# Two chained transformer blocks on one core: woven matmuls ahead of a pair's row products from row 290 on, another order of work before the first expert gather, a third norm buffer, and tables loaded early

## The reference

```python
def first_block(x, c, ctx, ...):               # x: 512 x 1024
    sh1, sc1, gt1, sh2, sc2, gt2 = ada_mod(c, ada_w, ada_b)
    ...
    o = jnp.concatenate([o_gdn, o_rwkv], axis=-1) @ w_out
    x = x + gt1 * o[:, n_ctx:]
    x = x + gt2 * peer_ffn(modulate(rms_norm(x, norm2_g), sh2, sc2), ...)
    return rms_norm(x, final_norm_g)

def peer_ffn(h, w_query, sub_keys, down, up):
    q = (h @ w_query).reshape(B, T, 8, 2, 128)          # 16 queries a token
    s = jnp.einsum('bthpd,hpkd->bthpk', q, sub_keys)    # 128 scores each
    s_top, i_top = lax.top_k(s, 16)
    ...                                                 # best 16 of 16 x 16 sums, 8 heads
    gate = jax.nn.softmax(best_s, axis=-1)              # 128 experts a token
    act = gelu(einsum('td,ted->te', h_blk, down[i_blk]))
    return einsum('te,ted->td', act * g_blk, up[i_blk]) # a block of 128 tokens
```

## Time and profile before

| | us |
|---|---|
| median of 3 runs | 3761.59 (3760.1 to 3765.12) |
| the profiled execution, its own time | 3768.46 |
| its span, first to last instruction | 3766.4 |
| PE busy | 3306.8 (88%) |
| DVE busy | 2408.0 (64%) |
| ACT busy | 1114.4 (30%) |
| POOL busy | 1014.9 (27%) |

### The profile page before, as it was taken

How to read it: one execution, slowest core, us unless ns; L and a number is a source line. 1 busy time by engine, 2 the same in 40 slices (tenths; PEclk the granted TensorE clock), 3 DMA queues, 4 the chain that set the end, 5 groups by cost and what they waited for, 6 DMA issues and landing times.

```text
span 3766.4 us, 59546 instructions
## 1 busy us (share of the span) xinstructions
PE 3306.8 (88%) x24177; PEld 1947.6 (52%) x24177; DVE 2408.0 (64%) x4781; ACT 1114.4 (30%) x2905; POOL 1014.9 (27%) x1021
## 2 busy tenths in 40 slices
PE   7998899899998876666567999999999998999998
PEld 4556666788876332222122333333368854468853
DVE  3865635687756766588777787764444147457765
ACT  2442212444422332333334344332222023410000
POOL 1024410345420333333342233323200000034432
PEclk8999999999999999777788999999999999999999
DMA  4147630000024999999999999989834421012233
GB/s 184 45 184 264 226 113 23 2 11 3 3 86 145 383 414 417 415 405 415 403 414 373 357 389 375 375 344 388 333 108 145 132 74 43 1 68 90 90 123 145
DMA packets 146412, 800.88 MB, mean 213 GB/s; under 512 B 13934, under 2 KB 33773, under 8 KB 62812
## 3 DMA queue, kind: packets, MB, share of 16 engines
q0 software_dynamic: 76048, 543.64, 36.1%
q1 hardware_dynamic: 68940, 251.34, 18.3%
q10 hardware_dynamic: 1152, 2.10, 0.1%
HBM read 794.92 MB, written 2.10 MB: 212 GB/s over the span
## 4 chain that ended last, share of the span: by engine, by line
PE 54%; DVE 13%; DMA 10%; ACT 4%; issue 2%; POOL 0%; DVEq 0%; POOLq 0%; ACTq 0%
PE bank L104 19%; PE bank L2721 8%; DMA row<-in_experts,idxs 7%; PE bank L3154 7%; PE bank L3170 4%; PE bank L4244 3%; DVE row L2914 3%; DMA wring<-in_experts,idxs 2%; PE bank L3946 2%; PE bank L2668 1%; PE bank L1108 1%; DVE wring L2914 1%; PE bank L1089 1%; PE bank L1880 1%; ACT cf L2811 1%
## 5 line engine op out<-in xcount | busy, mean ns | idle before, releaser
L2721 PE MATMUL bank<-row,dg 64*64 64x512 f32 x2920 | 431.8, 703 | 212.2 <-ACT dg L2817 211.8
L2914 DVE CUSTOM_DVE_ANT_0 row<-row,bank 128x1024 f32<-128x1024 f32 x365 | 445.6, 1221 | 192.4 <-DMA row<-in_experts,idxs 154.7
L2981 POOL DMA_INDIRECT row<-in_experts,idxs x365 | 362.3, 993 | 712.7 <-PE bank L2721 643.5
L2721 PEld LDWEIGHTS bank<-row,dg 64*64 64x64 f32 x2920 | 114.9, 148 | 470.6 <-issue 470.0
L3154 PE MATMUL bank<-s_hid,wring 128*128 128x512 f32 x704 | 327.3, 610 | 0.0
L104 PE MATMUL bank<-hT,wring 128*128 128x256 f32 (+1 forms) x864 | 286.6, 492 | 3.0 <-ACT sq L898 3.0
L2808 ACT ACTIVATE act<-dots 128x2 f32<-128x2 f32 x256 | 51.8, 203 | 710.6 <-DVE dots L2914 710.2
L2721 PE MATMUL bank<-wring,dg 64*64 64x512 f32 x1176 | 180.1, 708 | 91.0 <-ACT dg L2817 90.9
L2981 POOL DMA_INDIRECT wring<-in_experts,idxs x147 | 141.7, 964 | 368.7 <-PE bank L2721 264.3
L3154 PEld LDWEIGHTS bank<-s_hid,wring 128*128 128x128 f32 x704 | 129.0, 192 | 200.1 <-issue 199.3
L2914 DVE CUSTOM_DVE_ANT_0 wring<-wring,bank 128x1024 f32<-128x1024 f32 x147 | 179.5, 1221 | 81.0 <-DMA wring<-in_experts,idxs 67.5
(11 more groups left out here) (731 smaller groups left out, 6376.5 us busy)
## 6 DMA issues: line engine op xcount, KB each, us to landing
wring<-in_ffn_up SPq DMA_DIRECT2D x66, 1024.0 KB, 6.8
wring<-in_ada_w SPq DMA_DIRECT2D x64, 1024.0 KB, 6.6
wring<-in_ffn_down SPq DMA_DIRECT2D x32, 704.0 KB, 4.3
wring<-in_ffn_w_down SPq DMA_DIRECT2D x20, 1024.0 KB, 6.5
wring<-in_w_in SPq DMA_DIRECT2D x7, 2048.0 KB, 8.2
wring<-in_peer_w_query SPq DMA_DIRECT2D x8, 1024.0 KB, 25.6
wring<-in_attn_w_qkv SPq DMA_DIRECT2D x3, 2048.0 KB, 7.8
row<-in_experts,idxs POOLq DMA_INDIRECT x365, 9.9
```

Of the source, the lines that this page charges most:

```text
L2721: ins = pe.e.matmul(self.ks[t][64 * half:64 * half + 64, :], self.dg[u % 4][p, 0:64], row[p, 1024 + half * 512:1536 + half * 512], start=( ...
L2914: e.tensor_tensor_reduce(row, row, P.pairs[0], 1.0, 0.0, MUL, ADD, self.dots[:, g % 2, x:x + 1]).then_inc(*V.up("pg_dot", j))
L2981: e.indirect_dma_start(self.places[r], None, P.i["experts"], bass.IndirectOffsetOnAxis(ap=idu[:, b, j % 128:j % 128 + 1], axis=0)).then_in ...
```

## The change

It has three parts, which share no code.

**One: MixerOut.** PE turns only block 3 first, and does the w_out product of a block's half in two parts of 4 matmuls, the part of the first four input chunks (those of o_gdn) and that of the last four (out_pe's new argument `part`). Of block 2, half a column half stands ahead of the queries 0 to 7 (before: both halves), the rest behind them. DVE norms block 3 as before, then makes the first 8 choice steps, and only then adds block 2. Norms of the other blocks are split into `mean` and `normed`, and ACT's order goes with it. The query tiles get six places (an idle part of the constants, and y of the scan stage), so that all eight tiles are loaded without a place that waits for queries past the fourth tile.

**Two: Experts.pe.** For rows from 290 on, the woven work of a pair of rows stands ahead of the pair's row products; for rows before that, the steps of rest_pe of an even row move from behind the pair's products to ahead of them.

**Three: n10 and Qkv.** n10 has three buffers tmp (so that the third block needs none back), only two qkv units instead of four stand ahead of n10's turns, and the rest are followed by one turn each. The tables of the rotation and the gains have a place of their own and are loaded once the last block of the first stage is finished (pg_final 3), by POOL, which waited for the stage's begin before.

```diff
@@ MixerOut.dv
+        self.mean(dv, 3)
         self.normed(dv, 3)
         self.heads_dv(dv, 0)
+        choice, f = P.experts.choose(dv, 3, 0), self.first
+        for _ in range(8):
+            next(choice)
         self.added(dv, 2, 0)
+        next(choice)
         self.added(dv, 2, 1)
-        choice, f = P.experts.choose(dv, 3, 0), self.first
-        for _ in range(11):
+        for _ in range(2):
             next(choice)
         self.added(dv, 1, f)
...
+        self.mean(dv, 2)
         self.added(dv, 1, 1 - f)
         self.added(dv, 0, 1 - f)
-        for b in (2, 1, 0):
+        self.normed(dv, 2)
+        for b in (1, 0):
+            self.mean(dv, b)
+        for b in (1, 0):
             self.normed(dv, b)
@@ MixerOut.ac
         x.scores_ac(ac, 0, 7)
         x.rows_ac(ac, 0)
         x.weigh(ac, 3, 0)
+        self.squares(ac, 2)
+        self.root(ac, 2)
         for n in range(8, 16):
             x.query_ac(ac, 0, n)
             if n > 8:
                 x.scores_ac(ac, 0, n - 1)
+            if n == 8:
+                self.squares(ac, 1)
             if n == 9:
-                self.squares(ac, 1)
-            if n == 10:
                 self.squares(ac, 0)
-                self.root(ac, 2)
-            if n == 12:
                 self.root(ac, 1)
-            if n == 14:
                 self.root(ac, 0)
@@ MixerOut.out_pe
-    def out_pe(self, pe, ws, b, half):
+    def out_pe(self, pe, ws, b, half, part):
+
         P = self.P
         w, wb = ws[half]
-        k = P.bank(pe, "ro_o", half, b)
+        k = P.ps("ro_o", half, b) if part else P.bank(pe, "ro_o", half, b)
         pe.wait_ge(*P.at("wload", w))
-        pe.wait_ge(*P.at("free", "ro_T", b, 1))
...
+        pe.wait_ge(*P.at("free", "ro_T", b, part))
+        ins = mm(pe.e, k, [(self.oT[part][:, c, b * 128:(b + 1) * 128], wb[:, 4 * part + c, :]) for c in range(4)], start=(part == 0), stop=(part == 1))
+        if part:
+            ins.then_inc(*self.T.up("ro_o", half, b))
@@ Experts
-        self.wq = Tiles(P, "query_w", quarter[2:4] + [first[0], P.mem("wq", 2048)], 8)
+        self.wq = Tiles(P, "query_w", quarter[2:4] + [first[0], P.mem("wq", 2048), P.cst[:, P.idle:P.idle + 2048],
+                                                      P.rout.rs.y.rearrange("p b h i -> p (b h i)")], 8)
...
-        return 2 + n % 2 if n < 8 else n % 2
+        return (2, 3, 4, 2, 3, 4, 5, 2)[n] if n < 8 else n % 2
...
-        for n in range(16):
-            after = None if n < 2 or n in (8, 9) else n - 2
+        for n in (2, 0, 1, 3, 4, 5, 7, 6, 8, 9, 10, 11, 12, 13, 14, 15):
+            after = {3: 0, 4: 1, 5: 2, 7: 3}.get(n) if n < 10 else n - 2
...
-            if x % 2 == 0:
-                self.row_pe(pe, u)
-                self.row_pe(pe, u + 1)
             for _ in range(self.steps(u)):
                 next(rest, 0)
...
+            if u < self.BEHIND and x % 2 == 0:
+                self.row_pe(pe, u)
+                self.row_pe(pe, u + 1)
             P.around.pe(pe, u)
+            if u >= self.BEHIND and x % 2:
+                self.row_pe(pe, u - 1)
+                self.row_pe(pe, u)
+
+    BEHIND = 290
...
             elif r == 3:
-                po.wait_ge(*P.at("query_w_free", 6))
+                po.wait_ge(*P.at("query_w_free", 7))
@@ HiddenState, Tail.pe, Qkv
-        return self.tmps[n % 2], self.order[n - 2] if n >= 2 else None
+        return self.tmps[n % self.spare], self.order[n - self.spare] if n >= self.spare else None
...
-        P.cycle((1, 2, 3))
-        for u in range(1, P.qkv.ahead):
-            P.qkv.unit_pe(pe, u)
-        P.cycle((5, 6, 7, 4))
+        P.cycle((1,))
+        P.qkv.unit_pe(pe, 1)
+        P.cycle((5, 6, 7, 2, 3, 4))
         for b in (2, 3, 4):
             P.n10.turn_pe(pe, b)
...
-        super().po(po)
         i, e = self.P.i, po.e
+        po.wait_ge(*self.P.at("pg_final", 3))
...
-        for u in range(self.ahead, 14):
+        for u in range(2, 14):
             self.unit_pe(pe, u)
-            for _ in range(2 if u == self.ahead + 2 else 1):
-                self.turn(pe, turned)
-                turned += 1
-        for u in range(turned, 14):
+            self.turn(pe, u - 2)
+        for u in (12, 13):
             self.turn(pe, u)
```

More of the change, by code:

```diff
@@ L360, in plan @@
         self.top = hbase + 32960
-        self.n10 = HiddenState(self, 1, 0, "ffn0", "n10", "ffn0_down_x", 0, [5, 2, 3, 4])
+        self.n10 = HiddenState(self, 1, 0, "ffn0", "n10", "ffn0_down_x", 0, [5, 2, 3, 4], 3)
         self.top = low
@@ L2333, in added, with mean @@
         e.tensor_tensor(P.x[:, b, cs], P.x[:, b, cs], tp, ADD).then_inc(*V.up("x1", half, b))
+    def mean(self, dv, b):
+        st = self.st[:, 56 + 4 * b:60 + 4 * b]
+        dv.wait_ge(*self.P.at("pq_sq", b))
+        dv.e.tensor_scalar(st[:, 1:2], st[:, 0:1], 1.0 / D, 1e-6, MUL, ADD).then_inc(*self.V.up("pq_mean", b))
     def normed(self, dv, b):
@@ L2361, in ac @@
         x = P.experts
-        for b in self.BLOCKS:
-            self.turned_ac(ac, b, 0)
-        self.root_ac(ac, 2)
+        self.turned_ac(ac, 3, 0)
         ac.wait_ge(*P.at("ro_bonus", 0))
         self.turned_ac(ac, 3, 1)
+        self.root_ac(ac, 2)
         self.root_ac(ac, 1)
+        for b in (2, 1, 0):
+            self.turned_ac(ac, b, 0)
         self.turned_ac(ac, 2, 1)
+        self.squares(ac, 3)
+        self.root(ac, 3)
         for q in range(4):
@@ L2371, in ac @@
             e.activation(self.skT[:, 4 * q:4 * q + 4, :], v4(P.ps("pq_keys", q)), ACT.Copy).then_inc(*A.up("free", "pq_keys", q))
-        self.squares(ac, 3)
-        self.root(ac, 3)
         self.turned_ac(ac, 1, 1)
+        self.out_ac(ac, 3)
         self.root_ac(ac, 0)
-        self.out_ac(ac, 3)
-        ac.wait_ge(*P.at("ro_y", 0))
         for n in range(8):
             x.query_ac(ac, 0, n)
+            if n == 1:
+                ac.wait_ge(*P.at("ro_y", 0))
             if n:
                 x.scores_ac(ac, 0, n - 1)
-            if n == 3:
-                self.squares(ac, 2)
         self.turned_ac(ac, 0, 1)
@@ L2445, in pe @@
         self.gate_pe(pe, 3)
-        for b in self.BLOCKS:
-            self.turn_pe(pe, b, 0, P.ogdn[:, b])
+        self.turn_pe(pe, 3, 0, P.ogdn[:, 3])
         self.gate_pe(pe, 2)
+        self.gate_pe(pe, 1)
         ws = [P.weight("pe", 8, 512) for _ in range(2)]
@@ L2452, in pe @@
         self.heads_pe(pe, 3)
-        self.out_pe(pe, ws, 3, 0)
-        self.out_pe(pe, ws, 3, 1)
-        self.gate_pe(pe, 1)
+        for part in range(2):
+            for half in range(2):
+                self.out_pe(pe, ws, 3, half, part)
+        P.cycle((6, 7, 0, 3, 6, 7, 0, 6, 3, 7, 1))
+        for b in (2, 1, 0):
+            self.turn_pe(pe, b, 0, P.ogdn[:, b])
         self.heads_pe(pe, 2)
@@ L2474, in pe @@
                 x.scores_pe(pe, 0, n - 1)
-        P.cycle((6, 7, 0, 1))
+        P.cycle((6, 7, 0, 1, 0, 1))
         self.heads_pe(pe, 0)
@@ L2478, in pe @@
         x.scores_pe(pe, 0, 7, k)
-        self.out_pe(pe, ws, 1, f)
-        self.out_pe(pe, ws, 0, f)
+        self.out_pe(pe, ws, 2, 0, 1)
+        for b, half in ((2, 1), (1, f), (0, f)):
+            for part in range(2):
+                self.out_pe(pe, ws, b, half, part)
         T_.mark("wfree", ws[f][0])
-        self.out_pe(pe, ws, 1, 1 - f)
-        self.out_pe(pe, ws, 0, 1 - f)
+        for b, half in ((1, 1 - f), (0, 1 - f)):
+            for part in range(2):
+                self.out_pe(pe, ws, b, half, part)
         T_.mark("wfree", ws[1 - f][0])
@@ L2650, in sy @@
                 sy.wait_ge(*P.at("ro_T", 0, 0))
+            if n == 6:
+                sy.wait_ge(*P.at("ro_T", 0, 1))
             if n == 8:
@@ L3520, with __init__ @@
 class HiddenState(Stage):
-    def __init__(self, P, layer, which, before, name, made, shift=0, order=None):
+    def __init__(self, P, layer, which, before, name, made, shift=0, order=None, spare=2):
         super().__init__(P, name, before)
@@ L3527, in __init__ @@
         self.As = P.mem("As", 8)
-        self.tmps, self.st = [P.mem("tmp", 1024) for _ in range(2)], P.mem("st", 24)
-        self.order = order
+        self.tmps, self.st = [P.mem("tmp", 1024) for _ in range(spare)], P.mem("st", 24)
+        self.order, self.spare = order, spare
     def rows(self, b):
@@ L4500, in __init__ @@
         self.units = [(2, 0), (2, 1), (2, 5), (0, 5), (2, 2), (2, 3), (2, 4), (0, 2), (0, 3), (0, 4), (1, 5), (1, 2), (1, 3), (1, 4)]
-        self.ahead, self.w = 4, {}
+        self.w = {}
     def sy(self, sy):
```

12 lines of the change are left out of this document (5 added, 7 removed).

## The result

The changed kernel takes 3700.5 us (median of 4 runs, 3699.2 to 3703.2), the kernel before 3762.0 in the same comparison: a ratio of 0.9837 (95% interval 0.982 to 0.9854), 61.5 us less. The direction was right, the size was not.

The account below looks back on a forecast made before the run. Gathers were taken to bound 1250 to 2000 us, PE the woven stretch 2036 to 2718, neither MixerOut. −14.3 − 24 + 6.4 − 9.8 = −41.7 from 3768.5 gives 3727; that execution was 6.9 above the median, so 3720, range 3703 to 3744.

Parts of the forecast that it names:

- Part one, −14.3: MixerOut: first row products 14.3 us earlier, set by the last norms before the fifth gather, kept to 2036; bounds 8.3 and 16.
- the two waits on DVE: MixerOut: DVE waits 1.5 and 2.5 us for block 2's products, which now stand behind the queries.
- the first gather's own lead: MixerOut: indices 8.3 us earlier, at 1192.7; as a rival setting the time, 3726, chance 0.15.
- end of the queries (1212): MixerOut: queries 8 to 15 end at 1212 instead of 1227, without the 8.16 us wait for a tile.
- Part two, −24 + 6.4: Experts.pe, woven work ahead: 24 us gained from waits and lower clock, 6.4 lost behind the last row products.
- price at the end: Behind the last row products: later by 4.4 us, with PE waiting, and 2 for the lower clock; +6.4, bounds 0 and 8.
- The other twelve waits (17 us): Woven stretch: the rest of 19 PE waits for diagonals dg, said to be at other borders than an eviction and untouched.
- the seven: Woven stretch: PE waits of 2.43 to 3.42 us, 20.4 together, behind ACT's eviction and silu; all should vanish.
- 26 to 28 us: Woven stretch: gain that can be had from 20.4 us of vanished waits plus lower-clock losses; 24 was taken.
- The rival that they bind: Woven stretch: transfers bind there too, so PE is freed for nothing and the end's cost stays; 3744, chance 0.1.
- Part three, −9.8: n10 and qkv: no wait at the third turn, DVE starts units earlier, end at 3138 for 3148; bounds −4.3 and −13.
- The rival "more": Woven stretch and its end: all 19 waits shrink (6 us), the end costs nothing (10 us); 3704, chance 0.1.

Follow-up runs that it names:

- The fifth run: The kernel before, with gelu in place of silu in the context's convolution, so ACT loads no table there: 3743.3 us, ratio 0.9937.
- the sixth: The changed kernel, with gelu in place of silu in the context's convolution, so ACT loads no table there: 3702.9 us, ratio 0.9836.

## Why the prediction was wrong

**Part one, −14.3: right in size, with another last link.** Alone it gave 12.5, and 15 to 16 in the mean of the profiles. The first query and the two waits on DVE came near the forecast, and so did the first gather's own lead (8.3 forecast, 8.4 in the mean), which did not set the time. But the norms did not set it either. They were over at 1207.5, where 1213 to 1215 was forecast; the last scores, at 1210, came after them and held back the fourth gather and DVE's first dot product. The forecast's end of the queries (1212) was near this, so the sum did not suffer. One reading of a row was wrong without harm: 16 instructions (3.29 us) are one query, not two.

**Part two, −24 + 6.4: this step failed.** It measured −40.5 alone. Three steps of its gain were too small, the first also wrong in what it said; its price at the end was nearly right.

- "The other twelve waits (17 us) are at other borders than an eviction, which the shift does not touch." So they were put at nothing. Two of them stand at the begin, ahead of the stretch. Of the ten in it, the longest, 3.52 us, is at an eviction and a silu; it was there to be read, and the prediction reads the chain of one wait only. The row, and ACT ahead of it:

```profile
2331.28 3.69 PE L2721 MATMUL bank<-row,dg 64*64 64x512 f32 x16 [3.52 <-ACT dg L2817]
```
```profile
2326.32 1.28 ACT L3326 ACT_TABLE_LOAD   x1
...
2328.15 0.58 ACT L3321 ACTIVATE c_pad<-bank 128x512 f32<-128x512 f32 x1
2328.74 1.28 ACT L2808 ACT_TABLE_LOAD   x1
```

In its place the seven had the wait of 2.43 at 2183.97, where ACT had been idle and DVE came late, with the choice and a product of woven work (L3401) ahead of the dot product:

```profile
2183.97 1.09 PE L2721 MATMUL bank<-row,dg 64*64 64x512 f32 x8 [2.43 <-ACT dg L2817]
```
```profile
2180.62 0.69 DVE L3401 TENSOR_TENSOR s_gT<-s_gT,s_cv 128x512 f32<-128x512 f32 x1
2181.46 1.22 DVE L2914 CUSTOM_DVE_ANT_0 wring<-wring,bank 128x1024 f32<-128x1024 f32 x1
```

So the waits at silus were 21.5 us, and all seven are gone; the other ten were 9.8, and 2.8 are left. PE's idle time of the stretch fell by 28.6 us, where 20.4 was forecast. In seven of these ten (8.4 us) woven work on DVE stands ahead of the pair's dot product, as in this chain of before:

```profile
2614.63 0.45 PE bank L3185 x4
...
2615.11 0.42 DVE x L3504
...
2616.00 1.22 DVE row L2914
...
2618.01 0.36 ACT dg L2817
...
2618.51 1.50 PE bank L2721 x10
```

Woven work of PE ends (the turn L3185), DVE must add its result before it takes the pair's dot product, and the diagonal comes after that. It is the same pattern as the eviction: a follower engine has the woven result's work in its stream ahead of the next pair's. A lead of a whole pair covers most of it; the three waits that are left in the new order have DVE's woven work ahead of them too, together with its choice. The fifth run says the same from the other side: with the table switch away, half of the loss was still there in the old order, and the sixth that nothing of it was left in the new.

- The lower clock cost PE 10.4 us of busy time in the stretch, where I had counted 5.6 for the products and "some" for the up matmuls behind them. After the wait at 2119.20 the granted clock was 0.50 (the lower level, 1.2 GHz) to 2122.9, through the pair that I priced, and 0.72 in the 4 us of up matmuls behind it.
- From 26 to 28 us of these I then took 24, with the transfers as the reason. They moved 397 GB/s in the new order without stopping PE, at a share of 0.99. The rival that they bind is refuted. The Trainium skill, DMA: Bandwidth & Descriptors (Where 436 GB/s comes from), has about 358 GB/s as a core's limit from HBM; the stretches of after, with 397 and 411 on this one core, do not agree.
- The price at the end was nearly right: 4.1 us of wait for 4.4, and 3.1 for the lower clock instead of 2, so 7.2 in all for 6.4, within the bounds.

**Part three, −9.8: right in the sum.** Alone it gave 9.7, and the last turn came 10.0 us earlier counted from the first qkv unit; the forecast's own terms give 10.6 (3129.4 + 6.9 + 1.1 = 3137.4, which it rounded to 3138). But two of its reasons carry little: the early tables are worth 1.5 us and the third buffer 2.5 in the profiles, beside the new order of units, and nothing that the times show.

The rival "more" had the right sign, and its 3704 is near the 3700.5, but by luck in part. With its 10 us taken as the other waits and its 6 as the end's price, it gives part two a gain of 34, where the profiles have 43, and no price at the end, where they have 7.2: two errors that nearly cancel.

## What to carry to other kernels

When a busy engine alternates its own work with rows that depend on followers, list every wait, and for each ask which follower has the last piece's result ahead of it in its stream; here a lead of one unit of work covered nearly all that share this pattern, not only the dearest kind. Read the chain ahead of each wait before it is counted to a kind. Price a short wait with the clock behind it, by the busy time of a stretch and not by the next row: here the clock cost a third as much as the waits themselves. At the end of such a stretch part of the lead is paid back (7.2 us here), unless the last unit returns to the old order.

## What had not been expected

Executions differ by several us in a stretch with the same code: the first gather came 2.5 and 3.7 us earlier and 2.1 us later than in the profile of before in three kernels that do not change what stands before it. And in the stretch that PE fills, this core's transfers ran at 397 GB/s for 643 us beside a PE busy 640 of them.
